# A 31-tap convolution shared by ScalarE and GpSimd inside eight attention heads, with the heads' scores one weight block later

## The chip, the cores and the metric

One Trainium2 chip (trn2), one of its cores. The metric is the device time of one execution in microseconds. Engines: PE (TensorE), DVE (VectorE), ACT (ScalarE), POOL (GpSimd) and SP (SyncE, which here only starts loads).

## The reference, cut to what matters

The input has 256 tokens of 2048 features; all is float32. `first_block` (a recurrent and attention mixer, a gated MLP, an embedding gate) runs first and the change does not touch it. `second_block` is the part in question:

```python
h = rmsnorm(x, norm_g[l])
proj = h @ w_in[l]
(cv_a, cv_b, cv_gate, fq, fk, fv, f_logit, fox_gate, mq, mem_gate) = jnp.split(proj, SPLITS, axis=-1)

u = cv_a * jax.nn.sigmoid(cv_b)                       # 512 channels
u = causal_depthwise_conv(u, conv_w[l], conv_b[l])    # 31 taps, each channel by itself
u = jax.nn.silu(layernorm(u, conv_ln_g[l], conv_ln_b[l]))
y_conv = (u @ w_conv_pw[l]) * jax.nn.silu(cv_gate)

logf = jax.nn.log_sigmoid(f_logit.astype(jnp.float32) + b_f[l].astype(jnp.float32))
y_fox = fox_attention(fq, fk, fv, logf)               # 8 heads; bias = differences of cumsum(logf)
y_fox = y_fox * jax.nn.silu(fox_gate)
y_mem = memory_attention(mq, mk, mv) * jax.nn.silu(mem_gate)      # 4 heads
y = jnp.concatenate([y_conv, y_fox, y_mem], axis=-1)
x = x + y @ w_out[l]
```

## The kernel before

Features lie on the partitions, tokens (T = 256) along the free axis. A weight block is 128 output features by 2048 inputs, 1 MB. SP loads it into one of four slots of `stage`; ACT copies it to `whi` with its high half (`hi`, L429); DVE subtracts that from the block to get `wlo` (`lo`, L834), which lies over `stage`; PE multiplies (`whole`, L1602): for each of 16 cells one matmul of `whi` with both halves of the activations (512 columns, L1586) and one of `wlo` with the high half (256 columns, L1587). The sums lie in one of two banks `ps`. ACT copies half of the bank out (`evac`, L436), DVE adds the two halves (`add`, L840, which frees the bank through `out_free`) and scales the result (`scaled`, L848 and L850). A bank is taken again two blocks later, so PE's block n waits for the `add` of block n - 2 and for `lo` of its own weights. Each engine runs its instructions in the order in which the program has them; the semaphores alone tie the engines together.

The stage around the change, in order:

- **Conv stage.** Eight blocks give cv_a and cv_b; DVE writes their gated product to `upad` (L1242, counted by `u_ready`). PE then computes the forget gate's logits with 32 small matmuls (L1837).
- **The forget gate's chain.** DVE computes log-sigmoid, cumulative sum (`cc`, L1253) and the sum's three bf16 parts (L1246 to L1262), all on 48 partitions by 256, each operation waiting for the one before (`link`). ACT does an Exp and a Ln in between (L724, L726).
- **The convolution, on POOL.** One product of `upad`, shifted by the tap, with the tap's weights, 128x1024 (`tap_product`, L1543), and one addition into `uc` (L1559), for each of 31 taps in turn (L1549 adds the convolution's bias instead after tap 0), with no one waiting for it until the memory heads.
- **Eight gate heads** (`fox_head`: ACT L737, DVE L1274, PE L1850), one block each for query, key, value and gate, i.e. blocks u to u+3. PE: block 0; turn the softmax of the head before (`fox_turned`); block 1; weighted sum of the head before (`fox_out`); block 2; the scores (`masked_scores`, L1619, which wait for the query `fqT`, the key `fkT` and the two biases `cpos` and `cneg`); block 3; turn the values (into `ps_b`). DVE: for each block `add`, `lo` of the block three ahead, `scaled`; then bias, maxima and sign of the scores (L1295 to L1298), softmax, and the gate's x * sigmoid(x) with a reciprocal of 1.75 us (`logistic`, L857). Head 0 stands alone, heads 1 to 7 are a loop.
- **Four memory heads** of two blocks each (PE L1897 on). In them the layer norm of the convolution is done piece by piece: sums by POOL and PE (`uc_summed`, `usq_summed`), mean and square on DVE after head 0, `mu` and the inverse root at head 2, scaling and gain in the middle of head 3 (L1342 to L1344), ACT's sigmoid after the last head (L793). Then four blocks for cv_gate, with turning and sum of the last memory head between them, the pointwise product (`parts`), and the 16 blocks of w_out.

Of the kernel before, what the change touches and what calls it, by code (L numbers as in the profile page):

```python
# [19 lines left out]
ALU = mybir.AluOpType  # L20
# [81 lines left out]
def build(nc, a, out):  # L102
    with ExitStack() as ctx:
# [317 lines left out]
        def _(act):  # L421
# [314 lines left out]

            def fox_head(i, before=None):  # L737
# [12 lines left out]
                act.activation(fs[:, 0:P], fs[:, 0:P], ACT.Exp, bias=cols[:, 10:11], accum_out=cols[:, 12:13]).then_inc(s("fox_exp"), 1)  # L750
                act.activation(fs[:, P:3 * P], fs[:, P:3 * P], ACT.Exp, bias=cols[:, 11:12], accum_out=cols[:, 13:14]).then_inc(s("fox_exp"), 1)
# [5 lines left out]
                act.activation(fvtok[:, :, :], ps_b.rearrange("p (a b) -> p a b", a=2), ACT.Copy).then_inc(s("fvtok_ready"), 1)  # L757

# [13 lines left out]
            for n in range(MEM_HEADS):  # L772
# [4 lines left out]
                if n == 2:  # L777
                    norm(mu[:, :], "uc")
# [46 lines left out]
        def _(dve):  # L825
# [425 lines left out]
            dve.wait_ge(s("z_ln"), 1)  # L1251
            link(dve.tensor_tensor(z2[:, :], zf[:, :], z1[:, :], ALU.subtract))
            link(dve.tensor_tensor_scan(cc[:, :], one8[:, :], z2[:, :], 0.0, ALU.mult, ALU.add))  # L1253

            for n, (whole_c, left) in enumerate(((cc, z1), (z1, z2))):
                link(dve.tensor_copy(cpart[n], whole_c[:, :]))
                link(dve.tensor_tensor(left[:, :], whole_c[:, :], cpart[n], ALU.subtract))
            keeps = [fox_rows[:, 2 * HEADS + 2 + n:2 * HEADS + 3 + n] for n in range(PARTS)]
            link(dve.tensor_scalar(cc[:, :], z2[:, :], keeps[2], None, ALU.mult))
            for n in range(2):  # L1260
                link(dve.scalar_tensor_tensor(out=cc[:, :], in0=cpart[n], scalar=keeps[n], in1=cc[:, :],
                                              op0=ALU.mult, op1=ALU.add))  # L1262


# [9 lines left out]
            def fox_head(i, before=None):  # L1274
# [5 lines left out]
                scaled(u, 0, fqT[:, :], "fq_ready", factor=SCALE)  # L1280

# [24 lines left out]
                lo(G_FOX, i, 4, 6)  # L1306
                scaled(u + 3, 1, fgx[:, :], "fg_lin")
# [23 lines left out]
            for n in range(MEM_HEADS):  # L1331
                u = U_MEM + 2 * n
                if n == 2:
                    dve.wait_ge(*event("usq_summed"))
                    dve.tensor_scalar(mu[:, :], uc_square, 1.0 / (GROUPS * P), EPS, ALU.mult, ALU.add).then_inc(event("uc_ms")[0], 1)
# [3 lines left out]
                if n == 3:  # L1339

                    dve.wait_ge(*event("uc_norm"))
                    link(dve.tensor_tensor(uc[:, :, :], uc[:, :, :], by_mean, ALU.mult))  # L1342
                    for k in range(GROUPS):
                        dve.tensor_scalar(uc[:, k, :], uc[:, k, :], column("conv_ln_g", k), column("conv_ln_b", k),  # L1344
                                          ALU.mult, ALU.add).then_inc(s("cl_ready"), 1)
# [15 lines left out]
                if n == 0:  # L1361
# [4 lines left out]
                    dve.tensor_tensor(usq[:, :, :], uc[:, :, :], uc[:, :, :], ALU.mult).then_inc(s("usq_ready"), 1)  # L1366
            dve.wait_ge(s("cl_sig"), 1)
# [51 lines left out]
        def _(pool):  # L1419
# [119 lines left out]
            pool.wait_ge(s("u_ready"), GROUPS)  # L1539
            taps = vec[:, V["taps"]:V["taps"] + GROUPS * TAPS].rearrange("p (k t) -> p k t", k=GROUPS)  # L1540
            every = [P, GROUPS, T]

            def tap_product(dst, tap):  # L1543
                return pool.tensor_tensor(dst, upad[:, :, bass.ds(tap, T)],  # L1544
                                          taps[:, :, bass.ds(tap, 1)].to_broadcast(every), ALU.mult)

            tap_product(uc[:, :, :], 0).then_inc(s("tap_done"), 1)
            pool.wait_ge(s("tap_done"), 1)
            pool.tensor_tensor(uc[:, :, :], uc[:, :, :], column("conv_b_2", 0, GROUPS).unsqueeze(2).to_broadcast(every),  # L1549
                               ALU.add).then_inc(s("tap_done"), 1)  # L1550


            with pool.Fori(0, (TAPS - 1) // 2) as i:
                chain.enter(i, 2)
                for j, made in enumerate((usq, sg_c)):
                    pool.wait_ge(s("tap_done"), 2 * i + j + 1)
                    link(tap_product(made[:, :, :], 2 * i + j + 1))
                    pool.wait_ge(s("tap_done"), 2 * i + j + 2)
                    pool.tensor_tensor(uc[:, :, :], uc[:, :, :], made[:, :, :], ALU.add).then_inc(s("tap_done"), 1)  # L1559
# [460 lines left out]
```

## Time and profile before

| | |
|---|---|
| median of 3 runs | 1953.25 us (1953.09 to 1955.03) |
| the profiled execution | 1952.65 us, span 1950.9 us |
| mean granted clock of PE | 0.969 of 2.4 GHz |
| busy: PE, DVE, ACT, POOL | 93%, 71%, 46%, 36% of the span |
| convolution and eight gate heads | 1496.6 to 1761.1 us of the span |

Busy shares are means over stages with different limits, so they are read by stretch. An instruction's duration holds what it waited for inside, for instance for a port; what an engine waited for ahead of an instruction is its idle time. The clock is given as a share of 2.4 GHz for a stretch; 0.5 is the 1.2 GHz level, and values between are mixtures.

### The profile page before, as it was taken

The numbers are of one execution on the slowest core, as the hardware profiler recorded it, in microseconds if no ns is written. First come the engines' busy times: TensorE is split into PE (matmuls) and PEld (weight loads), VectorE is DVE, ScalarE is ACT, GpSimd is POOL, SyncE is SP. The second block draws the span as 40 slices with busy tenths as digits, with TensorE's granted clock in tenths as the row PEclk, the third lists the DMA queues.
The fourth block names the chain that finished last, engine by engine and source line by source line (L and its number), as shares of the span: only waits on it lengthen the run. The fifth ranks groups of instructions, "written<-read, shape, count | busy, mean of one in ns | idle before, by whom it ended". The sixth has DMA issues, their size and how long they took to land.

```text
span 1950.9 us, 29749 instructions
## 1 busy us (share of the span) xinstructions
PE 1823.6 (93%) x10284; PEld 1586.9 (81%) x10284; DVE 1394.6 (71%) x1633; ACT 901.9 (46%) x1160; POOL 709.1 (36%) x612
## 2 busy tenths in 40 slices
PE   5899999999969999999999999997999678899997
PEld 4688888887848888888888888886887567788886
DVE  7777777876767777777777544447777887778854
ACT  4444444454346555555555433335554222345532
POOL 3444444442972111111111122223543999500033
PEclk9899999999979999999999999998999789899998
DMA  6344444445624555455555555554554233344452
GB/s 250 120 154 169 152 171 163 160 166 193 224 86 165 182 191 188 180 191 190 179 190 180 181 182 190 187 184 150 193 186 167 77 121 115 133 162 168 157 191 108
DMA packets 50424, 326.49 MB, mean 167 GB/s; under 512 B 5840, under 2 KB 6480, under 8 KB 17744
## 3 DMA queue, kind: packets, MB, share of 16 engines
q1 hardware_dynamic: 50384, 325.96, 47.1%
q8 instruction: 25, 0.41, 0.1%
q14 instruction: 15, 0.12, 0.0%
HBM read 323.84 MB, written 2.10 MB: 167 GB/s over the span
## 4 chain that ended last, share of the span: by engine, by line
PE 79%; DVE 10%; POOL 5%; issue 4%; ACT 1%; DMA 1%; DVEq 0%; POOLq 0%; SPq 0%; ACTq 0%
PE ps L1586 49%; PE ps L1587 25%; DVE wlo L834 2%; PE ps_lev L1661 1%; DVE act_a L1073 1%; POOL sq L1478 1%; PE ps_sc L1625 1%; POOL lev_in L1459 1%; POOL mem_again L1427 1%; POOL lev_in L1455 1%; DVE act_a L877 1%; DVE fqT L850 1%; DVE cpos L1283 1%; DVE fgx L848 0%; PE ps_t L1615 0%
## 5 line engine op out<-in xcount | busy, mean ns | idle before, releaser
L1586 PE MATMUL ps<-act_a,whi 128*128 128x512 f32 x3136 | 1137.3, 403 | 56.9 <-DVE tmp L840 23.9
L1587 PE MATMUL ps<-act_a,wlo 128*128 128x256 f32 x3136 | 895.3, 285 | 0.0
L834 DVE TENSOR_TENSOR wlo<-stage,whi 128x2048 fp32r<-128x2048 f32 (+1 forms) x317 | 721.2, 2275 | 229.9 <-ACT whi L429 225.6
L1586 PEld LDWEIGHTS ps<-act_a,whi 128*128 128x128 f32 x3136 | 599.6, 191 | 201.4 <-issue 34.0
L429 ACT ACTIVATE whi<-stage 128x2048 fp32r<-128x2048 f32 (+1 forms) x317 | 570.9, 1801 | 120.2 <-DMA stage<-in_w_down 108.5
L1587 PEld LDWEIGHTS ps<-act_a,wlo 128*128 128x128 f32 x3136 | 600.8, 192 | 0.9
L1586 PE MATMUL ps<-big,whi 128*128 128x512 f32 x1600 | 569.2, 397 | 8.2 <-DVE big L1164 6.9
L1587 PE MATMUL ps<-big,wlo 128*128 128x256 f32 x1600 | 454.7, 284 | 0.0
L436 ACT ACTIVATE small<-ps 128x256 f32<-128x256 f32 x252 | 96.2, 382 | 592.5 <-PE ps L1587 592.3
L1586 PEld LDWEIGHTS ps<-big,whi 128*128 128x128 f32 x1600 | 303.2, 190 | 79.2 <-DVE big L1164 5.2
L1587 PEld LDWEIGHTS ps<-big,wlo 128*128 128x128 f32 x1600 | 303.6, 190 | 0.1
L840 DVE TENSOR_TENSOR tmp<-ps,small 128x256 f32<-128x256 f32 x212 | 89.6, 422 | 198.9 <-ACT small L436 192.0
L1521 POOL TENSOR_TENSOR upb<-tmp,rstd 128x256 f32<-128x256 f32 x88 | 76.5, 870 | 414.5 <-DVE tmp L840 400.3
L1455 POOL TENSOR_TENSOR lev_in<-qq,pfx 128x128 f32<-128x128 f32 x64 | 47.6, 744 | 221.6 <-DVE qq L979 217.2
L1479 POOL TENSOR_TENSOR acc<-acc,sq 128x256 f32<-128x256 f32 x63 | 100.2, 1590 | 5.0
L1478 POOL TENSOR_TENSOR sq<-y 128x256 f32 x16 | 11.7, 730 | 195.5 <-DVE y L840 195.5
L1478 POOL TENSOR_TENSOR sq<-h 128x256 f32 x31 | 19.0, 613 | 164.4 <-DVE h L1402 116.2
L1100 DVE SCALAR_TENSOR_TENSOR cy<-upb,vec,cy 128x256 f32<-128x256 f32 x88 | 64.4, 732 | 12.5 <-DVE cy L1098 12.2
L605 ACT ACTIVATE cy<-upb,vec 128x256 f32<-128x256 f32 x88 | 52.5, 596 | 4.0 <-POOL upb L1521 4.0
L1459 POOL TENSOR_TENSOR lev_in<-kk,sfx 128x128 f32<-128x128 f32 x64 | 49.1, 767 | 5.0
L1463 POOL TENSOR_TENSOR pfx<-pfx 128x128 f32<-128x128 f32 x56 | 46.9, 837 | 4.4
L1559 POOL TENSOR_TENSOR uc<-uc,usq 128x1024 f32<-128x1024 f32 x15 | 46.0, 3068 | 2.4 <-POOL usq L1544 2.4
(326 smaller groups left out, 1433.1 us busy)
## 6 DMA issues: line engine op xcount, KB each, us to landing
stage<-in_w_a SPq DMA_DIRECT2D x167, 1024.0 KB, 4.8
stage<-in_w_b SPq DMA_DIRECT2D x87, 1024.0 KB, 4.8
stage<-in_w_down SPq DMA_DIRECT2D x64, 704.0 KB, 4.0
h<-in_xT SPq DMA_DIRECT2D x8, 512.0 KB, 6.5
mem_raw<-in_memT SPq DMA_DIRECT2D x1, 2048.0 KB, 10.7
mem_again<-in_memT SPq DMA_DIRECT2D x4, 512.0 KB, 7.5
out<-o_out SPq DMA_DIRECT2D x4, 512.0 KB, 2.7
stage<-in_w_a SPq DMA_DIRECT2D x4, 256.0 KB, 7.0
```

The lines of the kernel that those rows point to most:

```text
L429: act.activation(whi[:, slot, 0:cells * P], stage[:, slot, 0:cells * P], ACT.Copy).then_inc(w_hi, 1)
L436: act.activation(small[:, b, :], ps[:, b, T:2 * T], ACT.Copy).then_inc(small_ready, 1)
L605: act.activation(cy[:, b, :], upb[:, b, 2:T + 2], ACT.Identity, scale=w[0], bias=w[1])\
L834: dve.tensor_tensor(wlo[:, slot, part], stage[:, slot, part], whi[:, slot, part].bitcast(F32), ALU.subtract).then_inc(w_lo, 1)
L840: dve.tensor_tensor(tmp[:, b, :] if dst is None else dst, ps[:, b, 0:T], small[:, b, :], ALU.add).then_inc(out_free, 1)
L1100: dve.scalar_tensor_tensor(out=cy[:, b, :], in0=upb[:, b, 0:T], scalar=w[0], in1=cy[:, b, :], op0=ALU.mult, op1=ALU.add).then_inc(s(done), 1)
L1455: link(pool.tensor_tensor(x1, q1, p1, ALU.mult))
L1459: pool.tensor_tensor(x0, k0, s0, ALU.mult).then_inc(s("lev_in_ready"), 1)
L1479: pool.tensor_tensor(total, total, sq, ALU.add).then_inc(step(done + "_acc", 0)[0], 1)
L1521: pool.tensor_tensor(upb[:, q % 2, 2:T + 2], tmp[:, q % 2, :], rstd[:, :], ALU.mult).then_inc(s("up_ready"), 1)
L1586: pe.matmul(ps[:, bank, :], whi[:, slot, c * P:(c + 1) * P], act, start=start, stop=False)
L1587: return pe.matmul(ps[:, bank, T:2 * T], wlo[:, slot, c * P:(c + 1) * P], act[:, 0:T], start=False, stop=stop)
```

## The change

- The convolution's products go to ACT: `first_taps` (tap 0 with the bias, four Identity activations of 128x256), then `tap_products`, four Copy activations of 128x256 each scaled by a column of weights, into `sg_c` and `usq` by turns. Two taps are made in head 0, four in each of the seven turns of the loop. POOL only adds (`add_tap`), each tap in two halves of 128x512. POOL waits for `product_made`; ACT waits for `product_added` before it overwrites a buffer of two taps ago.
- PE runs all four blocks of a head ahead of its scores; turning and sum of the head before come one block later. ACT and DVE follow that order.
- On DVE the softmax goes ahead of the gate's reciprocal and product, `add` and `scaled` of block 3 go ahead of the scores' bias and maxima, and the split of the head before goes behind the softmax. On ACT the softmax's exponentials go behind the block's high half, the gate's exponential and the values' copy.
- The second part of the forget gate's chain (`forget_gate`) goes behind the first `add`, `lo` and `scaled` of head 0.
- The convolution's mean is taken after memory head 1 instead of 0, the inverse root in head 3 instead of 2, and scaling and gain come behind the last memory head instead of in its middle. PE's column sums move with them.

```diff
             def fox_head(i, before=None):          # ACT
                 u = U_FOX + 4 * i
                 evac(u, 0, G_PG - U_PG)
                 hi(G_FOX, i, 4, 3)
-                if before is not None:
-                    fox_turned(before)
+                if before is None:
+                    first_taps()
+                else:
+                    tap_products(before, 3)
                 evac(u + 1, 1, G_PG - U_PG)
                 hi(G_FOX, i, 4, 4)
+                if before is None:
+                    tap_products(0, 1)
+                else:
+                    fox_turned(before)
+                    tap_products(before, 4)
                 evac(u + 2, 0, G_PG - U_PG)
                 hi(G_FOX, i, 4, 5)
-                if before is not None:
+                if before is None:
+                    tap_products(0, 2)
+                else:
                     fox_out(before)
-                wait(act, "fox_max", i + 1)
...
+                    tap_products(before, 5)
                 evac(u + 3, 1, G_PG - U_PG)
                 hi(G_FOX, i, 4, 6)
                 wait(act, "fg_lin", i + 1)
                 act.activation(fge[:, :], fgx[:, :], ACT.Exp, scale=-1.0).then_inc(s("fg_exp"), 1)
...
+                wait(act, "fox_max", i + 1)
...
+                if before is not None:
+                    tap_products(before, 6)
```

```diff
+            def first_taps():
+                act.wait_ge(s("u_ready"), GROUPS)
+                for k in range(GROUPS):
+                    act.activation(uc[:, k, :], upad[:, k, 0:T], ACT.Identity, scale=tap_column(0, k),
+                                   bias=column("conv_b_2", k)).then_inc(s("product_made"), 1)
+
+            def tap_products(i, j):
+
+                made = (sg_c, usq)[j % 2]
+                if not (isinstance(i, int) and j <= 2):
+                    act.wait_ge(s("product_added"), i * 8 + 2 * (j - 2))
+                for k in range(GROUPS):
+                    act.activation(made[:, k:k + 1, :], upad[:, k:k + 1, bass.ds(4 * i + j, T)], ACT.Copy,
+                                   scale=tap_column(4 * i + j, k)).then_inc(s("product_made"), 1)
...
+            def add_tap(i, j):                     # POOL
+
+                made = (sg_c, usq)[j % 2]
+                for half in range(2):
+                    pair = slice(2 * half, 2 * half + 2)
+                    pool.wait_ge(s("product_made"), i * 16 + 4 * j + 2 * half + 2)
+                    if not (isinstance(i, int) and j == 1):
+                        pool.wait_ge(s("product_added"), i * 8 + 2 * (j - 1) + half - 1)
+                    pool.tensor_tensor(uc[:, pair, :], uc[:, pair, :], made[:, pair, :], ALU.add).then_inc(s("product_added"), 1)
+
+            add_tap(0, 1)
+            add_tap(0, 2)
+            with pool.Fori(0, HEADS - 1) as n:
+                for j in range(3, 7):
+                    add_tap(n, j)
```

```diff
             def fox_head(i, before=None):          # DVE
...
                 scaled(u, 0, fqT[:, :], "fq_ready", factor=SCALE)
+                if before is None:
+                    forget_gate()
...
                 if before is not None:
                     fox_gated(before)
+                add(u + 3, 1)
+                scaled(u + 3, 1, fgx[:, :], "fg_lin")
                 wait(dve, "fsc_ready", i + 1)
                 wait(dve, "fp_turned", i)
                 link(dve.tensor_tensor(fs[:, 0:3 * P], ps_sc[:, 0:3 * P], bias_fox, ALU.add))
...
-                if before is not None:
-                    fox_split(before)
-                add(u + 3, 1)
+                lo(G_FOX, i, 4, 6)
                 wait(dve, "fox_exp", 2 * i + 2)
...
-                lo(G_FOX, i, 4, 6)
-                scaled(u + 3, 1, fgx[:, :], "fg_lin")
+                if before is not None:
+                    fox_split(before)
                 logistic(fge[:, :], "fg_exp", i + 1)
```

```diff
             def fox_head(i, before=None):          # PE
                 u = U_FOX + 4 * i
                 whole(G_FOX, i, 4, 0, u, 0, act_a)
+                whole(G_FOX, i, 4, 1, u + 1, 1, act_a)
                 if before is not None:
                     fox_turned(before)
-                whole(G_FOX, i, 4, 1, u + 1, 1, act_a)
+                whole(G_FOX, i, 4, 2, u + 2, 0, act_a)
                 if before is not None:
                     fox_out(before)
-                whole(G_FOX, i, 4, 2, u + 2, 0, act_a)
+                whole(G_FOX, i, 4, 3, u + 3, 1, act_a)
                 wait(pe, "c_ready", 2 * i + 2)
...
-                whole(G_FOX, i, 4, 3, u + 3, 1, act_a)
```

```diff
+            dve.wait_ge(*event("uc_norm"))         # DVE, behind the last memory head
+            link(dve.tensor_tensor(uc[:, :, :], uc[:, :, :], by_mean, ALU.mult))
+            for k in range(GROUPS):
+                dve.tensor_scalar(uc[:, k, :], uc[:, k, :], column("conv_ln_g", k), column("conv_ln_b", k),
+                                  ALU.mult, ALU.add).then_inc(s("cl_ready"), 1)
             dve.wait_ge(s("cl_sig"), 1)
             dve.tensor_tensor(uc[:, :, :], uc[:, :, :], usq[:, :, :], ALU.mult).then_inc(s("cs_ready"), 1)
```

## Rows read from the trace of the kernel before

**Rows 1.** The page: engine totals, as busy us, share of the span, instructions.

```profile
PE 1823.6 (93%) x10284; PEld 1586.9 (81%) x10284; DVE 1394.6 (71%) x1633; ACT 901.9 (46%) x1160; POOL 709.1 (36%) x612
```

**Rows 2.** By stretch: length; busy (count) PE, PEld, DVE, ACT, POOL; clock; DMA.

```profile
1496.70:1539.00 42.30, 21.36 (x103) 17.73 (x104) 41.84 (x25) 9.83 (x10) 41.11 (x17) 0.76 0.20 75
1539.00:1573.50 34.50, 28.30 (x145) 23.73 (x144) 27.97 (x25) 10.68 (x15) 33.55 (x12) 0.90 0.34 122
...
1705.30:1730.40 25.10, 25.10 (x145) 21.71 (x144) 17.86 (x26) 11.04 (x17) 0.00 (x0) 1.00 0.43 164
...
1539.00:1678.40 139.40, 112.86 (x574) 94.64 (x573) 115.70 (x103) 43.68 (x63) 135.92 (x45) 0.89 0.34 121
...
1496.70:1761.20 264.50, 217.03 (x1138) 183.96 (x1139) 213.60 (x211) 87.53 (x124) 183.77 (x64) 0.90 0.35 123
```

**Rows 3.** Waits, 1489 to 1700 us: who for whom, total, times, longest.

```profile
PE ps_sc L1624 <- DVE fkT L848: 22.7, 5, 5.2
...
PE ps L1586 <- DVE tmp L840: 22.4, 5, 16.9
```

**Rows 4.** DVE by line, a slow head (1573.5 to 1608.6), then a quiet one.

```profile
L834 DVE TENSOR_TENSOR wlo<-stage,whi 128x2048 fp32r<-128x2048 f32 x4 | 12.4, 3112 | 0.0
...
L840 DVE TENSOR_TENSOR tmp<-ps,small 128x256 f32<-128x256 f32 x4 | 1.7, 417 | 5.3 <-ACT small L436 4.7 <-DVE fge L1309 0.6
...
L834 DVE TENSOR_TENSOR wlo<-stage,whi 128x2048 fp32r<-128x2048 f32 x4 | 9.2, 2290 | 3.3 <-ACT whi L429 3.3
```

**Rows 5.** DVE in order of time, the forget gate's chain: start, duration.

```profile
1497.16 0.39 DVE L1247 TENSOR_SCALAR zf<-zf,bfox 48x256 f32<-48x256 f32 x1
...
1504.02 2.01 DVE L1252 TENSOR_TENSOR z<-zf,z 48x256 f32<-48x256 f32 x1
```

**Rows 6.** PE in order of time: first cells of the first and third block.

```profile
1496.61 0.50 PE L1586 MATMUL ps<-act_a,whi 128*128 128x512 f32 x1
...
1525.02 0.76 PE L1586 MATMUL ps<-act_a,whi 128*128 128x512 f32 x1 [16.93 <-DVE tmp L840]
```

**Rows 7.** POOL in order of time.

```profile
1541.24 2.38 POOL L1559 TENSOR_TENSOR uc<-uc,sg_c 128x1024 f32<-128x1024 f32 x1 [0.16 <-POOL sg_c L1544]
1543.57 1.91 POOL L1544 TENSOR_TENSOR usq<-upad,vec 128x1024 f32 x1
...
1567.73 8.28 POOL L1559 TENSOR_TENSOR uc<-uc,usq 128x1024 f32<-128x1024 f32 x1 [0.16 <-POOL usq L1544]
...
1683.35 1.29 POOL L1563 TENSOR_TENSOR sg_c<-uc 128x512 f32<-128x512 f32 x1
```

**Rows 8.** The chain that ended last, in order of time: scores of two heads.

```profile
1704.09 0.42 PE ps_sc L1625 x2
...
1754.20 0.42 PE ps_sc L1625 x2
```

**Rows 9.** ACT's activations of 128x256: two page rows, one line of the stage before.

```profile
L436 ACT ACTIVATE small<-ps 128x256 f32<-128x256 f32 x252 | 96.2, 382 | 592.5 <-PE ps L1587 592.3
...
L605 ACT ACTIVATE cy<-upb,vec 128x256 f32<-128x256 f32 x88 | 52.5, 596 | 4.0 <-POOL upb L1521 4.0
...
L688 ACT ACTIVATE act_a<-h,vec x16: 496/498/511, 1367.8 to 1450.5; - x12, 128x256 fp32r<-128x256 f32 x4
```

**Rows 10.** After the last memory head: DVE, ACT and PE in order of time.

```profile
1812.72 1.22 DVE L1342 TENSOR_TENSOR uc<-uc,mu 128x1024 f32<-128x1024 f32 x1
1813.97 1.38 DVE L1344 TENSOR_SCALAR uc<-uc,vec 128x256 f32<-128x256 f32 x4
...
1822.58 0.42 DVE L1360 TENSOR_TENSOR fge<-fge,fgx 128x256 f32<-128x256 f32 x1
...
1819.91 1.07 ACT L793 ACTIVATE usq<-uc 128x1024 f32<-128x1024 f32 x1
...
1823.99 0.58 ACT L766 ACTIVATE fpT<-ps_t 128x512 f32<-128x512 f32 x1
...
1827.75 0.59 PE L1887 MATMUL bank_a<-fpT,fvtok 128*128 128x256 f32 x2
```

More of the change, by code:

```diff
@@ L735, in fox_out, with tap_column @@
                 act.activation(xs_y[:, bass.ds(GROUPS + n, 1), 0:T], fo[:, :].unsqueeze(1), ACT.Copy).then_inc(s("fo_hi"), 1)
+            def tap_column(tap, k):
+                return vec[:, bass.ds(V["taps"] + k * TAPS + tap, 1)]
+            def first_taps():
[10 more added lines that the diff above has]
+                                   scale=tap_column(4 * i + j, k)).then_inc(s("product_made"), 1)
             def fox_head(i, before=None):
@@ L757, in fox_head @@
                 act.activation(fvtok[:, :, :], ps_b.rearrange("p (a b) -> p a b", a=2), ACT.Copy).then_inc(s("fvtok_ready"), 1)
+                wait(act, "fox_max", i + 1)
+                act.activation(fs[:, 0:P], fs[:, 0:P], ACT.Exp, bias=cols[:, 10:11], accum_out=cols[:, 12:13]).then_inc(s("fox_exp"), 1)
+                act.activation(fs[:, P:3 * P], fs[:, P:3 * P], ACT.Exp, bias=cols[:, 11:12], accum_out=cols[:, 13:14]).then_inc(s("fox_exp"), 1)
+                if before is not None:
+                    tap_products(before, 6)
             fox_head(0)
@@ L776, in _ @@
                 memory_turned(n - 1) if n else fox_turned(HEADS - 1)
-                if n == 2:
+                if n == 3:
                     norm(mu[:, :], "uc")
@@ L1250, in _, with forget_gate @@
             link(dve.tensor_scalar(zf[:, :], zf[:, :], 0.0, None, ALU.min))
[L1251 to L1262, printed above, removed]
+            def forget_gate():
+                dve.wait_ge(s("z_ln"), 1)
+                link(dve.tensor_tensor(z2[:, :], zf[:, :], z1[:, :], ALU.subtract))
+                link(dve.tensor_tensor_scan(cc[:, :], one8[:, :], z2[:, :], 0.0, ALU.mult, ALU.add))
+                for n, (whole_c, left) in enumerate(((cc, z1), (z1, z2))):
+                    link(dve.tensor_copy(cpart[n], whole_c[:, :]))
+                    link(dve.tensor_tensor(left[:, :], whole_c[:, :], cpart[n], ALU.subtract))
+                keeps = [fox_rows[:, 2 * HEADS + 2 + n:2 * HEADS + 3 + n] for n in range(PARTS)]
+                link(dve.tensor_scalar(cc[:, :], z2[:, :], keeps[2], None, ALU.mult))
+                for n in range(2):
+                    link(dve.scalar_tensor_tensor(out=cc[:, :], in0=cpart[n], scalar=keeps[n], in1=cc[:, :],
+                                                  op0=ALU.mult, op1=ALU.add))
             def fox_gated(n):
@@ L1332, in _ @@
                 u = U_MEM + 2 * n
-                if n == 2:
+                if n == 3:
                     dve.wait_ge(*event("usq_summed"))
@@ L1338, in _ @@
                 lo(G_MEM, 0, 0, 2 * n + 3)
[L1339 to L1345, printed above, removed]
                 add(u + 1, 1)
@@ L1536, in _ @@
                              lambda i: pool.wait_ge(s("h3_ready"), i + 1), "h3", None)
[L1539 to L1559, printed above, removed]
-                chain.leave((TAPS - 1) // 2)
-            pool.wait_ge(s("tap_done"), TAPS + 1)
+            def add_tap(i, j):
[11 more added lines that the diff above has]
+                    add_tap(n, j)
+            pool.wait_ge(s("product_added"), 2 * (TAPS - 1))
             link(pool.tensor_tensor(sg_c[:, 0:2, :], uc[:, 0:2, :], uc[:, 2:4, :], ALU.add))
@@ L1903, in _ @@
                 turn(ps_b[:, P:T], mkv[:, MEM_HEADS + n, P:T], "mv_turned")
-                if n == 1:
+                if n == 0:
+                    column_sums(ps_lev[:, 0, 0, :], [sg_c[:, 2, :]], lambda n: event("uc_sum"), "uc_summed")
+                if n == 2:
                     column_sums(ps_lev[:, 1, 0, :], [usq[:, 0, :]], lambda n: event("usq_sum"), "usq_summed")
```

5 lines of the change are left out of this document (1 added, 4 removed).

## The prediction, made before the change was run

> **What bounds the kernel now.** Start with the page's engine totals [rows 1]: PE is busy for 93% of the span, so a change pays only where PE waits or runs slow. Next read busy time and clock by stretch [rows 2]. From 1496.7 to 1761.2 us eight gate heads run. A head in its quiet form (1705.3 to 1730.4) takes 25.1 us, PE is busy in all of it, the granted clock is 1.00 (2.4 GHz), and POOL does nothing. Four heads before it take 34.5 to 35.1 us (139.4 in all; the first is shown), with the clock at 0.89 to 0.90 and POOL busy nearly throughout: that is the convolution. The first 42.3 us are worse, PE busy for 21.4 and the clock at 0.76. Third, the waits [rows 3]: PE waits for two things, fkT (what the scores need, 22.7 us) and DVE's additions out of the output bank (22.4 us, 16.9 of it at once). DVE in its turn stands 5.3 us in a slow head for ScalarE's copy out of the bank [rows 4], which waits for PE. So the two take turns: PE stands before the scores, then the fourth block runs, then DVE stands until it is done.
>
> Why is DVE late? In the four slow heads it is busy 115.7 us where four quiet heads make 4 x 17.9 = 71.4 [rows 2]: 44.3 us are waiting inside instructions. The gate's chain shows it most plainly [rows 5]: an operation on 48x256 takes 0.39 us with POOL idle and 2.01 with POOL at work, and from 1504.0 until the addition that frees PE at 1525.0 [rows 6] the gate's cumulative sum and splits hold DVE. POOL's instructions in these heads are an addition of 2.38 us and a product of 1.91 by turns [rows 7]. 22 of each is 94 us of POOL's own work, so each microsecond of it costs DVE 44.3/94 = 0.47.
>
> What perfect heads would save. The quiet period is (1754.20 - 1704.09)/2 = 25.06 us [rows 8]. Seven of those, and a head 0 that has nothing to turn or sum for a predecessor (about 1.0 us less), make 199.5 us. The stage takes 264.5 [rows 2]. The difference, **65.0 us**, is 47.5 of PE idle (264.5 - 217.0) and about 17.5 of slow clock [rows 2]. A quiet head keeps PE busy all the time, so this is the ceiling, and no reordering below can gain beyond it. The loads keep up: a quiet head has the same four of 1 MB in 25.1 us, at a DMA share of 0.43 [rows 2].
>
> **The change part by part.**
>
> *Products to ScalarE.* POOL loses 31 products and the bias addition, and keeps 30 additions, each in two halves of 128x512. A half should take 1.29 us, what the one addition of that size took [rows 7]; half of a whole one, 1.19, is the lower bound, and waiting comes on top (up to the 5.9 us of the third rival). A loop turn holds eight: 10.3 us of POOL instead of all of it. At 0.47 that costs DVE 4.8 us a head, so DVE needs 17.9 + 4.8 = 22.7 of 25.1 us. ScalarE gains 16 products a head. No row has such an operation in this stage; the nearest is a Copy scaled by a column, 0.50 us [rows 9]. 16 x 0.50 = 8.0 on top of 11.0 [rows 2] makes 19.0 of 25.1. The bounds are 0.38 (a plain copy of this width) and 0.60 (scaled and biased by columns) [rows 9]: 17 to 21 us, which fits either way. What waits behind them on ScalarE is an evacuation. A block takes about 5.7 us (two from 1496.6 to 1508.1 [rows 6]); evacuation 0.3, high half 1.9, products 1.6 to 2.0 make 3.8 to 4.2, so the next evacuation is not late. Cost: **0**, covered by PE; without that cover up to 8 us a head.
>
> *The scores a block later.* PE now runs all four blocks and then the scores, so keys and cumulative sum have 5.7 us more, and DVE no longer stands behind the fourth block. PE's work is the same. In return the softmax's DVE work of head i reaches into the first block of head i+1. Counted from the start of a head: the fourth block ends at 23.3, scores at 24.6; DVE's parts, all of them within its 17.9: bias, maxima and sign 1.8 -> 26.4; low half 2.2 (2.29 with the overlap taken off [rows 4]) -> 28.6; softmax and split 1.3 -> 29.9; gate 2.5 -> 32.4; the first addition of the next head is possible at 31.1 and so done at 32.8. PE needs it for its third block, at 36.7. Of the 3.9 us in hand POOL can take two half additions (2.6). Further on the slacks are similar: the second addition done at 41 at worst against 42.7, the low half for the next head 43 against 50. The turning of the old head's weights also moves a block later, with the wait of ScalarE (fpT) and PE (output): weights ready at 29.5, needed at 36.7. Cost: **0**.
>
> *Softmax ahead of the sigmoid; products and ScalarE's exponentials reordered.* The same work by the same instructions. ScalarE's exponentials now stand behind the next high half and the values' copy (about 2.8 us after the evacuation at 23.3), which is when the maxima are ready. Cost 0.
>
> *The gate's chain into head 0.* Ten linked operations. They no longer delay the first addition, since that comes before them, and POOL cannot start before ScalarE has made two products of tap 1. PE's first block ends at 1502.2 as before; evacuation, high half and four first products carry ScalarE to 1506.5, second evacuation and high half to 1510.3, so POOL starts at about 1511.2. DVE: addition 1503.1, low half to 1506.7, fqT 1507.1, then ten times 0.45 (0.42 and a gap) = 4.5 -> 1511.6, biases 0.7 -> 1512.3, second addition 1512.7. PE needs it at 1513.5. With two half additions of POOL in between it is 1515.3. The unhindered price of the scan stands in no row; it can be 0.4 like its neighbours or 2.8 as it was with POOL in the way. I take a stall of **1.5 us** there, with 0 and 4 as ends (4 if PE drops to its 1.2 GHz level there, as the 0.76 of this stretch shows it did [rows 2]).
>
> *The norm moved back.* Mean and square one memory head later cost nothing: they fill gaps of DVE like those they leave. But the scaling now stands behind the last memory head's gate, at 1823.0: 1.2 + 1.4 us [rows 10] -> 1825.6, then ScalarE's sigmoid 1.1 -> 1826.7 (before, it ran at 1819.9 [rows 10]). Behind it wait the evacuation (possible at about 1822), a high half of 1.9 and the turned weights of the last head, ready at 1829.4 instead of 1824.6. PE wants them at 1827.8 [rows 10]. Cost: **+1.6 us**, ends 0 and 4. The pointwise product's input is done near 1837 and wanted at 1841: covered by the two blocks that remain.
>
> Sum: -65.0 + 1.5 + 1.6 = **-62 us**. Against the profiled execution (1952.65 us with a span of 1950.9) that is 1890.7; the median shown is 0.6 above it, so 1891.
>
> **The rivals.**
>
> *DVE becomes the bound.* If POOL's halves fall on DVE in full, a head costs 17.9 + 10.3 = 28.2 us instead of 25.1. Seven heads: 22, less 4 of slack = 18 more, 1909; a PE that waits also drops to its lower level, which adds up to 1.6 us each time. For it: the halves are released just when ScalarE has made a high half, and that is when DVE starts its low half of 2.3 us. Against it: the measured 0.47, and DVE's reads of the banks, which showed no waiting (0.417 us in a slow head, where a low half had grown from 2.29 to 3.11) [rows 4]. The Trainium skill (SBUF — State Buffer, Who interferes with whom) says the shared port pair is held for a whole instruction by whoever comes first and the other blocks fully. That is this rival's rule; by it alone the sum would be 1909, by the rows 1891.
>
> *The order of PE and DVE is good but the convolution still drags.* Heads at about 30 us, the slow ones' mean of 34.9 less PE's wait for fkT (22.7 / 5 = 4.5 [rows 3]): (30.4 - 25.1) x 7 = 37, 1928. It would need POOL's new load to weigh as much as the old, for which I see no row.
>
> *Slower than before.* POOL can be kept out: five of its instructions took over 8 us instead of 1.9 or 2.4, such as the one at 1567.7 [rows 7], about 5.9 us of waiting while DVE ran back to back. ScalarE now waits for POOL (product_added) with high halves and evacuations queued behind, so a starved addition reaches PE. 60 half additions in 264.5 us is 4.4 us each: from that mean on the kernel is slower than before. If each waited 5.9 us the stage would take 60 x 7.2 = 432 us, 167 more, about 2120. Against: a tap may be late by a whole block before ScalarE stops, and DVE has gaps in every block of a quiet head, where POOL gets in.
>
> **How the numbers follow.** PE-bound heads, 1887 to 1898: 60%. DVE-bound heads, 1898 to 1915: 26%. Heads dragged, 1915 to 1949: 9%. Within 0.2% of before: 2%. Slower: 3%. 0.2% is about what a measurement of this kernel tells from no change. The range 1886 to 1914 takes in the first two, 85%, and all ends of the unknown terms. Faster 95%, same 2%, slower 3%.
>
> **What would show it.** Right: head period near 25.1 with the clock at 1.00 from head 1 on; DVE busy 22 to 23 us and ScalarE 19 per head; POOL's halves near 1.3 us with a few longer; scores of head 0 near 1520 and the stage done near 1697 to 1698; gate operations of 0.4 us; a PE wait of about 1.6 us at the last memory head's output. Wrong: a period of 27 to 28 with DVE never idle (first rival); long POOL halves with ScalarE waiting for them (third). A saving above 66 us would mean that I missed something outside this stage.

## The result

The changed kernel takes **1902.2 us** (median of 4 runs, 1902.0 to 1903.0) where the kernel before, run again on the same chip, takes 1953.7 (1953.1 to 1955.0): ratio 0.9736, 95% interval 0.9719 to 0.9753. That is 51.5 us less. The forecast was 1891, 62 less; the time lies inside its range of 1886 to 1914, but some 11 us of the gain are missing, and the question of the rest of this text is where they went.

The profiled execution took 1903.01 us, with a span of 1901.2. The page's totals, beside [rows 1]:

```profile
PE 1812.0 (95%) x10284; PEld 1578.2 (83%) x10284; DVE 1357.9 (71%) x1633; ACT 951.9 (50%) x1284; POOL 629.0 (33%) x610
```

Busy time by stretch, with the columns of [rows 2]: head 0, heads 1 and 2, one period among the five later heads, the first memory head.

```profile
1496.70:1521.50 24.80, 24.80 (x140) 20.77 (x138) 18.04 (x27) 15.53 (x24) 9.85 (x4) 1.00 0.41 133
1521.50:1546.80 25.30, 25.30 (x146) 21.84 (x146) 19.47 (x25) 15.99 (x30) 9.66 (x6) 1.00 0.45 165
1546.80:1573.50 26.70, 25.37 (x145) 21.70 (x144) 23.46 (x27) 17.53 (x33) 10.62 (x9) 1.00 0.45 158
...
1599.51:1625.97 26.46, 25.31 (x144) 21.64 (x143) 22.33 (x26) 17.42 (x33) 13.69 (x9) 1.00 0.42 157
...
1705.80:1723.10 17.30, 14.94 (x78) 12.88 (x78) 15.50 (x20) 9.15 (x16) 6.29 (x6) 0.90 0.33 118
```

The stage that took 264.5 us [rows 2] takes 208.6 (1497.1 to 1705.7). Its clock is 1.00 throughout, and there is no wait for the key any more [rows 3]. But from head 2 on a head takes 26.5 us and not 25.1, and PE is idle in it for 1.2. What it waits for, in order of time on PE (start, duration; in brackets idle time before it and what ended it); two of the six such waits, then the one in the first memory head with cells behind it, then one after the last:

```profile
1559.59 0.50 PE L1610 MATMUL ps<-act_a,whi 128*128 128x512 f32 x1 [1.33 <-DVE tmp L870]
...
1612.59 0.50 PE L1610 MATMUL ps<-act_a,whi 128*128 128x512 f32 x1 [1.15 <-DVE tmp L870]
...
1713.74 0.90 PE L1639 MATMUL ps_t<-ident,fs 128*128 128x128 f32 x3 [2.36 <-DVE fs L1338]
...
1715.09 0.63 PE L1610 MATMUL ps<-act_a,whi 128*128 128x512 f32 x1
...
1717.00 0.39 PE L1610 MATMUL ps<-act_a,whi 128*128 128x512 f32 x1
...
1777.96 0.67 PE L1911 MATMUL bank_a<-fpT,fvtok 128*128 128x256 f32 x2 [1.52 <-issue]
```

`L870` is `add`: from head 2 on the third block of each head waits for DVE's first addition of that head. These waits of 1.15 to 1.33 us leave the clock at 1.00. The cells after the wait of 2.36 us at 1713.7 take 0.63 us each until 1717, with the clock at 0.50, the 1.2 GHz level. The addition's evacuation was done long before. This is DVE in order of time, from block 3's addition of one head to the first addition of the next:

```profile
1623.34 0.41 DVE L1298 TENSOR_TENSOR fo<-bank_a,fge 128x256 f32<-128x256 f32 x1
1626.21 0.42 DVE L870 TENSOR_TENSOR tmp<-ps,small 128x256 f32<-128x256 f32 x1 [2.45 <-ACT small L436]
1626.67 1.42 DVE L878 TENSOR_TENSOR fgx<-tmp,rstd 128x256 f32<-128x256 f32 x1
...
1631.86 1.13 DVE L1337 TENSOR_SCALAR fs<-fs,cols 128x128 f32<-128x128 f32 x1
1632.91 1.40 DVE L1338 TENSOR_SCALAR fs<-fs,cols 128x256 f32<-128x256 f32 x1
...
1634.88 1.75 DVE L887 RECIPROCAL fge<-fge 128x256 f32<-128x256 f32 x1
1636.67 1.36 DVE L1342 TENSOR_TENSOR fge<-fge,fgx 128x256 f32<-128x256 f32 x1
1638.57 0.42 DVE L870 TENSOR_TENSOR tmp<-ps,small 128x256 f32<-128x256 f32 x1 [0.53 <-ACT small L436]
```

and ScalarE, then POOL, in the same stretch (an `x2` of POOL is the two halves of one tap):

```profile
1623.90 0.42 ACT L735 ACTIVATE big<-fo 128x256 f32 x1 [3.13 <-DVE fo L1298]
1624.22 1.69 ACT L752 ACTIVATE usq<-upad,vec 128x256 f32 x4
1625.82 0.36 ACT L436 ACTIVATE small<-ps 128x256 f32<-128x256 f32 x1
...
1632.08 0.38 ACT L436 ACTIVATE small<-ps 128x256 f32<-128x256 f32 x1
...
1625.27 2.53 POOL L1578 TENSOR_TENSOR uc<-uc,usq 128x512 f32<-128x512 f32 x2 [4.55 <-ACT usq L752]
1631.51 2.65 POOL L1578 TENSOR_TENSOR uc<-uc,sg_c 128x512 f32<-128x512 f32 x2 [3.71 <-ACT sg_c L752]
1635.22 2.53 POOL L1578 TENSOR_TENSOR uc<-uc,usq 128x512 f32<-128x512 f32 x2 [1.06 <-ACT usq L752]
```

DVE first stands idle for 2.45 us, because PE now does block 3 ahead of the scores and nothing else stands ahead of that block's addition in DVE's program. The block ends at 1624.7, and a copy out of the bank (L436) can follow 0.1 us behind a block's end, as the one at 1637.69 does. But this one comes only at 1625.8, 1.0 us late: four products (tap 5) stand ahead of it on ScalarE, and they stand behind a copy of `fo` for which ScalarE had waited 3.13 us. Then DVE has fourteen instructions in a row, and four of them, each beside a POOL addition, take 1.42, 1.13, 1.40 and 1.36 us. In head 0 the same kind of scaled product took 0.41 (`fkT`), and the other three, standing clear of POOL, took 0.29, 0.35 and 0.42. That is 3.8 us of waiting inside. DVE's L1338, for one, ends at 1634.31, 0.15 us after POOL's tap at 1634.16. The turn of the loop adds 0.5: the profile names ScalarE for it, which had been done since 1632.5, but the same 0.53 us stand there in the second experiment, where another instruction comes first. So the addition that was possible at 1632.5 is made at 1638.6.

### The profile page after: what moved, and what is told of

It reads as the page before. It is cut to its first block, busy times and chain, and to the rows that moved or that the text cites. A ratio compares the mean times of both kernels' runs of the same rounds, so it can differ in the third digit from the quotient of the medians.

```text
span 1901.2 us, 30010 instructions
## 1 busy us (share of the span) xinstructions
PE 1812.0 (95%) x10284; PEld 1578.2 (83%) x10284; DVE 1357.9 (71%) x1633; ACT 951.9 (50%) x1284; POOL 629.0 (33%) x610
## 4 chain that ended last, share of the span: by engine, by line
PE 80%; DVE 8%; POOL 5%; issue 4%; ACT 2%; DMA 1%; DVEq 0%; POOLq 0%; ACTq 0%; SPq 0%
PE ps L1610 50%; PE ps L1611 26%; PE ps_lev L1685 1%; POOL sq L1509 1%; DVE act_a L1103 1%; DVE wlo L864 1%; POOL mem_again L1458 1%; POOL lev_in L1490 1%; POOL lev_in L1486 1%; DVE act_a L907 1%; DVE fge L887 1%; DVE fs L1338 1%; ACT whi L429 0%; POOL sfx L1493 0%; DVE tmp L870 0%
## 5 line engine op out<-in xcount | busy, mean ns | idle before, releaser
L864 DVE TENSOR_TENSOR wlo<-stage,whi 128x2048 fp32r<-128x2048 f32 (+1 forms) x317 | 711.4, 2244 | 227.0 <-ACT whi L429 222.6
L436 ACT ACTIVATE small<-ps 128x256 f32<-128x256 f32 x252 | 96.4, 382 | 540.3 <-PE ps L1611 540.2
L870 DVE TENSOR_TENSOR tmp<-ps,small 128x256 f32<-128x256 f32 x212 | 89.4, 421 | 190.4 <-ACT small L436 185.6
L1578 POOL TENSOR_TENSOR uc<-uc,usq 128x512 f32<-128x512 f32 x30 | 42.9, 1451 | 110.0 <-ACT usq L752 110.0
L1578 POOL TENSOR_TENSOR uc<-uc,sg_c 128x512 f32<-128x512 f32 x30 | 59.8, 2013 | 48.3 <-ACT sg_c L752 48.3
```

What stands on the lines that cost most here:

```text
L436: act.activation(small[:, b, :], ps[:, b, T:2 * T], ACT.Copy).then_inc(small_ready, 1)
L864: dve.tensor_tensor(wlo[:, slot, part], stage[:, slot, part], whi[:, slot, part].bitcast(F32), ALU.subtract).then_inc(w_lo, 1)
L870: dve.tensor_tensor(tmp[:, b, :] if dst is None else dst, ps[:, b, 0:T], small[:, b, :], ALU.add).then_inc(out_free, 1)
L1578: pool.tensor_tensor(uc[:, pair, :], uc[:, pair, :], made[:, pair, :], ALU.add).then_inc(s("product_added"), 1)
```

## The experiments

All are compared with the kernel before on the same chip; times are medians, and the head period is the distance of the same matmul in neighbouring heads. First three tests of what makes the first addition late, and one half of the change by itself.

**POOL's additions made small** (most of the convolution's sum left out):

```diff
-pool.tensor_tensor(uc[:, pair, :], uc[:, pair, :], made[:, pair, :], ALU.add)
+pool.tensor_tensor(uc[:, pair, 0:2], uc[:, pair, 0:2], made[:, pair, 0:2], ALU.add)
```

> The changed kernel with POOL's sixty additions cut to 2 of 256 columns each (most of the convolution's sum is left out; products, waits and order stay). Theory L (late chain): heads take 26.5 us instead of 25.1 because DVE's chain from block 3's evacuation to the next head's first addition is too long, 3.9 us of it waits for POOL's port. Without them: period 25.1, DVE busy 17.9 a head, 6 x 1.4 = 8.5 us saved and 1 to 2 at the first memory head, 1892 +- 2. Theory D (DVE's load as a whole is the bound): the same 25.1. Theory S (ScalarE's longer program is the bound): period stays 26.5, 1902.

Measured 1889.6 (0.967, 0.9654 to 0.9686), 12.6 us less than the change. One head:

```profile
1596.05:1621.12 25.07, 25.07 (x144) 21.63 (x144) 17.71 (x26) 17.38 (x33) 5.14 (x8) 1.00 0.46 167
```

PE is never idle, DVE is busy for 17.7 us, and ScalarE as long as before (17.4). S falls: the longer program of ScalarE alone costs nothing. What remains is POOL's use of the port, by its place (L) or by its sum (D).

**The next head's first addition ahead of split and gate:**

```diff
+                add(u + 4, 0)
                 if before is not None:
                     fox_split(before)
                 logistic(fge[:, :], "fg_exp", i + 1)
```

(with the head's own `add(u, 0)` left to head 0, and that of memory head 0 left out.)

> The changed kernel with one DVE instruction moved: the first addition of the next head goes ahead of the old head's split and gate (about 3.5 us earlier). L: the chain to that addition is shorter by 3.5 us, which is more than the 1.4 it is late, so period 25.1 to 25.3, DVE busy unchanged at 22.3, total 1894 +- 2. D: DVE's load is the same, period stays at 26.5, 1902. S: 1902.

Measured 1900.4 (0.9728, 0.9712 to 0.9744): next to nothing. The lateness went one place further. PE, and the window from one such wait to the next:

```profile
1668.46 0.50 PE L1613 MATMUL ps<-act_a,whi 128*128 128x512 f32 x1 [0.90 <-DVE tmp L870]
```

```profile
1642.24:1668.46 26.22, 25.32 (x143) 21.71 (x144) 22.98 (x27) 17.45 (x33) 10.71 (x8) 1.00 0.45 160
```

It is now the head's fourth block that waits, for the second addition, and the period is 26.2. L as I had it, one late instruction, is wrong. And the wait in the first memory head grew from 2.36 to 3.14 us, which takes back part of what the heads gained.

**Tap 5's products behind block 3's evacuation and high half:**

```diff
                     fox_out(before)
-                    tap_products(before, 5)
                 evac(u + 3, 1, G_PG - U_PG)
                 hi(G_FOX, i, 4, 6)
+                if before is not None:
+                    tap_products(before, 5)
```

> The changed kernel with ScalarE's four products of tap j = 5 put behind block 3's evacuation and high half, instead of ahead. L: the evacuation comes 0.9 us earlier, so the chain does, period 25.6, 6 x 0.9 = 5 us and up to 1 more at the first memory head: 1897 +- 2. D: 1902, as the load is the same.

Measured 1900.5 (0.9727, 0.9711 to 0.9743), and all of it outside the heads: PE's wait in the first memory head fell from 2.36 to 0.57 us, while the period stayed at 26.5. The evacuation did come earlier, but tap 5's additions, which had fallen partly into DVE's idle time, now met the softmax and the gate, so the chain lost on DVE what it gained on ScalarE:

```profile
1633.22 1.51 DVE L1303 TENSOR_TENSOR big<-fo,big 128x256 f32 x1
1634.66 1.38 DVE L887 TENSOR_SCALAR fge<-fge 128x256 f32<-128x256 f32 x1
```

**Order of the heads alone**, the convolution all on POOL as before (gate's chain and norm in the change's places).

> The changed kernel with the convolution as before, all on POOL; order of the heads, place of the gate's chain and of the norm as in the change. If the order removes the turns that PE and DVE take: five or six slow heads at about 30 us instead of 34.8, first head 8 us shorter, 1922 +- 6. If the order only helps where POOL is light: heads stay at 34 to 35, 1945 or more.

Measured 1937.3 (0.9916, 0.99 to 0.9933): 16.7 less than before, halfway between my two numbers. A slow head takes 30.1 to 30.7 us instead of 34.8, PE and DVE no longer take turns, and DVE is nearly full, busy for 28.5 of 30.2 us:

```profile
1616.60:1646.76 30.16, 27.09 (x143) 22.94 (x144) 28.53 (x27) 11.00 (x16) 29.37 (x10) 0.94 0.39 142
```

But head 0 gained little: PE waited 20.6 us for the second addition, because the gate's chain now stood ahead of that one, with POOL at work.

**The shared convolution alone**, heads and gate's chain in the old order, norm in its new place: PE, DVE and ScalarE run `fox_head` as the kernel before has it, with `tap_products` after the first, second and third high half and at the end.

> The kernel before with only the convolution shared by ScalarE and POOL and the norm moved back; heads and the gate's chain in the old order. In quiet heads of before the key was ready 1.2 us ahead of the scores, and POOL's halves now cost DVE 2 to 3 us ahead of it. Expected: PE waits 1 to 2 us for the key in each of seven heads, period 26.5 to 27.5, the gate's chain undisturbed (operations of 0.4 us), total 1906 +- 5. If the order of the heads is what carries the gain: above 1925.

Measured **1896.1** (0.971, 0.9693 to 0.9727), 6 us better than the whole change. The old order's wait for the key is 0.5 us in most heads, 1.0 in one and nothing in another:

```profile
1643.21 0.21 PE L1646 MATMUL ps_sc<-cneg,cpos 48*128 48x128 bf16 x1 [0.52 <-issue]
```

```profile
1617.59:1643.21 25.62, 25.11 (x143) 21.67 (x144) 20.76 (x26) 17.16 (x33) 14.77 (x9) 1.00 0.44 164
```

So the parts don't add: order alone -16.7, sharing alone -57.7, both -51.5 (each with the norm in its new place; the order includes the gate's chain in its new place). With the convolution on POOL the new order is worth 17 us; with it shared, it costs 6. I had expected neither sign nor size.

**POOL's additions whole** (one of 128x1024 a tap instead of two halves), in the changed kernel.

> The changed kernel with POOL's additions whole (128x1024, one per tap instead of two halves). L with a port held per instruction: a DVE instruction that meets one waits up to 2.4 us instead of 1.3, but half as often, and the addition starts only after all four products (0.8 us later). POOL's own work is the same, so DVE busy stays 21.5 to 22.5 a head and the time within 1902 +- 3. If what counts is the longest single wait: period over 27, 1906 or more.

Measured 1916.7 (0.9815, 0.9797 to 0.9832): the second of the two answers. The heads take 27.9 to 29.5 us, the longer ones in part at the lower clock (0.94 to 0.95 in them). One of the short ones:

```profile
1650.36:1678.44 28.08, 25.31 (x144) 21.65 (x144) 24.85 (x27) 17.41 (x34) 10.39 (x4) 1.00 0.42 151
```

**POOL's additions in quarters** (four of 128x256), in the changed kernel.

> The changed kernel with POOL's additions in four pieces of 128x256 for each tap instead of two of 128x512. One addition of 128x256 took 0.74 us in the kernel before, so POOL has 4 x 0.74 = 3.0 us of its own work a tap instead of 2.5. Whole additions made the head 28 to 29 us. If the length of a single wait is what makes DVE late: a wait of at most 0.75 us, DVE busy 21 a head, period 25.1 to 25.6, 1895 +- 2. If the number of meetings counts as much: DVE as busy as with halves (22.3), period 26.5, 1902 +- 1.5; if POOL's total work decides: over 1904.

Measured 1892.8 (0.969, 0.9674 to 0.9706), 9.4 us better than halves and near the first of the three answers. PE waits 0.33 us in every second head. Two heads:

```profile
1585.23:1635.94 50.71, 50.38 (x287) 43.30 (x287) 41.23 (x53) 34.75 (x65) 30.79 (x32) 1.00 0.46 165
```

Undisturbed, whole, halved (the change) and quartered additions cost POOL 2.4, 2.6 and 3.0 us a tap; with the first experiment they make a row. DVE busy in a head: 17.7 us with additions of two columns (0.2 us at the shortest, the row below), 20.6 with quarters, 22.3 with halves, 24.9 with whole ones. What DVE loses, 2.9, 4.6 and 7.1 us, grows with the length of a single addition (0.74, 1.3, 2.4 us) and not with POOL's sum, which falls from quarters to whole ones. The first experiment's row for half of its additions, nanoseconds as shortest, median and longest:

```profile
L1578 POOL TENSOR_TENSOR uc<-uc,usq x30: 201/216/3055, 1512.5 to 1697.5; 128x4 f32<-128x4 f32 x30
```

**Turning and sum of the last gate head a step later** in memory head 0 (PE's part):

```diff
-                memory_turned(n - 1) if n else fox_turned(HEADS - 1)
+                if n:
+                    memory_turned(n - 1)
                 whole(G_MEM, 0, 0, 2 * n + 1, u + 1, 1, act_a)
-                memory_out(n - 1) if n else fox_out(HEADS - 1)
+                memory_out(n - 1) if n else fox_turned(HEADS - 1)
...
+                if n == 0:
+                    fox_out(HEADS - 1)
```

> The changed kernel with one thing moved in memory head 0: the last gate head's softmax is turned after block 1 and its weighted sum taken after the memory scores, as the change does in gate heads. Theory: PE now waits there for DVE's softmax 2.4 us and loses 1.1 more to its 1.2 GHz level; both go: 1899 +- 1, granted clock 1.00 in the first memory head. Rival: the wait only moves to the next thing that DVE does late (query or addition of memory head 0): 1902.

Measured 1900.5 (0.9733, 0.9716 to 0.9751). The wait of 2.36 us is gone, and one of 1.44 for DVE's query (`DVE fqT`) ahead of the memory scores is there instead: between my two answers. The gain of 1.7 is inside the interval.

**The sigmoid behind the next evacuation**, high half and turned weights; DVE's product with it behind the first gate block's addition:

```diff
-            act.wait_ge(s("cl_ready"), GROUPS)
-            act.activation(usq[:, :, :], uc[:, :, :], ACT.Sigmoid).then_inc(s("cl_sig"), 1)
...
                     memory_turned(MEM_HEADS - 1)
+                    act.wait_ge(s("cl_ready"), GROUPS)
+                    act.activation(usq[:, :, :], uc[:, :, :], ACT.Sigmoid).then_inc(s("cl_sig"), 1)
```

> The changed kernel with ScalarE's sigmoid of the convolution put behind the next evacuation, high half and turned weights, and DVE's product with it behind the first gate block's addition. Theory: PE's wait of 1.5 us at the last memory head's sum goes: 1900.5 +- 0.7. Rival: the pointwise product's input comes so much later that PE waits for it instead: 1902 or more.

Measured 1900.5 (0.9732, 0.9715 to 0.975). The 1.52 us wait at the last memory head's sum is in no row of this run; the place is shown, the 1.7 us are within the interval. DVE's part of the edit is not in the cut above.

**The gate's chain in its new place, with the old order of the heads and the shared convolution.**

> The kernel with the shared convolution and the heads in the old order, and now the forget gate's second part in the place where the change has it (behind head 0's first addition, low half and query). With POOL idle while the chain runs in its old place, the place is worth nothing: 1896 +- 1.5. If the place carried part of the gain: 1893 or less, if it delays the key of head 0: 1898 or more.

Measured 1897.7 (0.9712, 0.9697 to 0.9727) against 1896.1: no gain from the place. PE's wait for the key of head 0 grew from 0.51 to 2.29 us. Once POOL starts later than the chain, there is nothing to protect it from.

**Four moves at once in the new order**: the first addition ahead, tap 5 behind the evacuation, the later turning, the sigmoid behind.

> The changed kernel with four things moved at once: the next head's first addition ahead of split and gate, tap 5's products behind block 3's evacuation, the last turning a block later, the sigmoid behind the next evacuation. Theory C (the cycle): with the scores behind all four blocks DVE stands before block 3's addition and then has all its work for the head in one piece, so a single move only hands the lateness to the next addition; the period stays at 26 to 26.3 and only the places outside the gate heads mend: 1896 +- 2. If the moves add up in the heads too: period 25.1 to 25.5, 1891 or less.

Measured **1889.9** (0.9675, 0.966 to 0.969), 12.3 us better than the change and the best of the kernels that compute the whole convolution. My theory C, that moves only hand the lateness on, is wrong too. PE has no wait in heads 1 to 7; one head:

```profile
1596.71:1621.78 25.07, 25.07 (x145) 21.63 (x144) 23.12 (x27) 17.27 (x33) 15.31 (x8) 1.00 0.46 166
```

DVE is busy for 23.1 of the 25.1 us, more than in the changed kernel, and still in time. So D, DVE's load as a whole, is out as well.

```profile
1603.39 0.41 DVE L874 TENSOR_TENSOR tmp<-ps,small 128x256 f32<-128x256 f32 x1
1603.73 1.18 DVE L1306 TENSOR_TENSOR big<-fo,big 128x256 f32 x1
1604.84 1.38 DVE L890 TENSOR_SCALAR fge<-fge 128x256 f32<-128x256 f32 x1
...
1613.65 0.41 DVE L874 TENSOR_TENSOR tmp<-ps,small 128x256 f32<-128x256 f32 x1
```

The first addition stands ahead of the two waits for the port that the single move of tap 5 had put in front of it. The second addition, for which PE had waited 0.9 us when the first alone was moved, now comes 18.3 us after the scores' start instead of 20.0: block 3 is copied out earlier, and its scaled product takes 0.42 us and no longer 1.42. It is done at 1614.1, and the fourth block starts at 1614.7. As I read it, two deadlines were missed by about a microsecond each, and each move mended one. That the two moves inside the heads do it, and not the two outside, follows from where they act; the pair wasn't run by itself.

**The same mending in the old order**: sigmoid behind, the convolution's sum on PE a block later, tap 5 behind block 3's evacuation.

> The kernel with the shared convolution and the heads in the old order, with three small moves: the convolution's sigmoid behind the next evacuation (1.5 us of PE's wait), PE's sum of the convolution one block later (0.9 us), tap 5's products behind block 3's evacuation and high half (evacuation 1.1 us earlier; the head's wait of 0.5 us goes if that was its cause). Theory C: 1891.5 +- 1.5, period 25.1 to 25.6. If tap 5's additions do harm in their new place, as they did in the new order: 1894 +- 1.

Measured 1906.8 (0.9764, 0.975 to 0.9777), 10.7 us worse than without the three, and far above both answers. Of them only tap 5 lies in the heads, and the heads are what got longer (26.9 to 29.9 us, at a clock of 0.95); tap 5 wasn't moved by itself. DVE, on its way to the key that the scores wait for:

```profile
1609.06 1.51 DVE L880 TENSOR_TENSOR fgx<-tmp,rstd 128x256 f32<-128x256 f32 x1
...
1611.07 0.82 DVE L888 TENSOR_SCALAR fge<-fge 128x256 f32<-128x256 f32 x1 [0.49 <-ACT fge L785]
...
1613.71 1.39 DVE L1341 TENSOR_TENSOR fge<-fge,fgx 128x256 f32<-128x256 f32 x1
...
1618.17 1.52 DVE L882 SCALAR_TENSOR_TENSOR fqT<-tmp,rstd 128x256 f32<-128x256 f32 x1
1619.61 1.38 DVE L1315 TENSOR_SCALAR cpos<-cc,fox_rows 48x256 bf16<-48x256 f32 x1
```

Five waits in that chain. Before the move the same five instructions took 0.42, 0.29, 0.66, 1.53 and 1.38 us: 2.3 us less in all. And tap 5's additions had begun at a moment when DVE stood idle for 1.4 us, and cost it 0.3:

```profile
1624.21 2.81 POOL L1576 TENSOR_TENSOR uc<-uc,usq 128x512 f32<-128x512 f32 x2 [4.34 <-ACT usq L752]
```

The same move helped in one order, beside the first addition's, and went with a loss in the other. By these rows what decides is which DVE instructions the additions meet, and whether PE waits for these.

## Why the prediction was right, and where it was wrong

**The time fell into the second class of the forecast.** 1902 lies in the class "DVE-bound heads, 1898 to 1915", given 26%, and not in the one with 60%, "PE-bound heads". The range holds it because it takes in both.

**The ceiling held.** It said that at most 65 us were to be had. The best complete kernel here has 63.7 (1953.6 - 1889.9) with a head period of 25.07, where 25.06 was forecast.

**DVE's cost of POOL held as a sum, in part by luck.** Forecast: 0.47 us per microsecond of POOL's own work, so 4.8 a head and DVE at 22.7. Measured: 22.33, where it is 17.86 with POOL idle [rows 2]. But 0.47 is no constant of the kernel: against the 17.7 us of the first experiment, quarters cost DVE 0.25 us per microsecond of POOL's own work, halves 0.45 and whole additions 0.74. Nothing here shows why the mean of the kernel before should fit the halves; I count it as luck. ScalarE's products were cheaper than assumed, 1.70 us for four, and it is busy for 17.4 and not 19 us a head. The first experiment shows that this cost nothing by itself.

**The step that failed is the cost of 0 for the scores a block later.** The prediction followed this very chain, from the fourth block to the first addition at "32.8 against 36.7", and found 3.9 us in hand, of which POOL could take 2.6. It took 3.8: six halves are released while the chain runs, and four of its instructions each met one, where the sum had allowed for two. The evacuation was 1.0 late because of tap 5's products. The prediction had reckoned ScalarE by its load, 3.8 to 4.2 us a block, and not with the 3.13 us for which it stands before `fo`, ahead of these products. And the turn of the loop took 0.5. Together 5.3 against 3.9, so 1.4 us a head; measured are waits of PE of 1.15 to 1.33 us and a period of 26.5 instead of 25.1, and 8.9 us over the seven periods (184.3 against 175.4). The average of 0.47 was used for the load, but a chain has to be priced with what can meet it. And the rule that was put down as the first rival's fits better than I allowed: the Trainium skill (SBUF — State Buffer, Who interferes with whom) says that the one who comes second blocks fully, until the instruction ends. The trace agrees: the four instructions waited 0.84 to 1.05 us each, and quarters, halves and whole additions cost 2.9, 4.6 and 7.1 us a head. The rival's sum, all of POOL's 10.3 us on DVE, did not come: 4.6 did, since some halves ran where DVE stood idle or was in an instruction that did not slow down, as the reciprocal, which took 1.75 us with a half beside it and without.

It also missed what the new order takes away. In the old order the scores come ahead of the fourth block, so DVE has softmax and gate to do while that block runs. In the new one it stands for 2.45 us and then has them all in one piece. The prediction counted PE's gain from this order and called its price 0.

**The first memory head was left out.** There the last gate head's turning still comes after one block and not two, as PE's new order has it elsewhere; the softmax was not ready. From its first block to the next head's it took 17.6 us, where the first experiment, without this wait, took 13.6. These 4.0 us, 2.36 of them idle and the rest mostly cells at the lower clock, had no term in the sum.

**Head 0: forecast 1.5 us of waiting, measured none.** The gate's operations took 0.28 to 0.50 us and the scan 0.68. A half addition did get in the way once (`cpos`, 1.26 us), but the second addition was done at 1513.8, just in time for the fourth block at 1514.0; with a second half in the way it would have been late. The forecast of the scores at about 1520 was right (1519.7).

**The norm moved back: forecast 1.6, measured 1.52** of idle time, at the named place, by the named path.

The sum is then: 62 forecast, less 8.9 for the periods, less 4.0, plus 1.5 = 50.6. Measured are 51.5 between the medians and 49.7 between the spans of the two profiled executions.

**The rivals.** The first (DVE becomes the bound) came nearest in time, 1909 against 1902 where the forecast said 1891, but its mechanism was only half right: DVE is not full in any head, at 22.3 of 26.5 us. It is late at one point. The third needed additions of 4.4 us in the mean and did not come near: 30 of them took 1.45 us, 30 took 2.01.

**Attribution.** The forecast gave the gain to both parts in one sum. The runs give it all to the sharing, which is worth 57.7 us alone (with the norm's new place), and the new order as it stands takes 6 of them back; with its two moves inside the heads it is the best run here. The gate's place shows no gain: 1.6 us the other way, with executions that overlap.

## What to carry over

When two engines share a port, price the contention twice: as a mean for the load, and, for a chain that has a deadline, by counting the instructions of the other engine that can be released while it runs, each at its full length. Cut the side instructions short and release them where the other engine stands idle; here their sum mattered less than their length and place. Before an order is changed to remove a wait, look at which work ran under the block that moves, and test the parts of a change one by one: two good parts here made a worse kernel than one, until the second was mended.

## What the runs showed that was not expected

- Additions in quarters cost POOL more (0.74 us each, 3.0 a tap, against 2.4 whole), but DVE 2.9 us a head instead of 7.1.
- The port's waits lie in POOL's time too. An addition of two columns takes 0.2 us, but up to 3.06 where DVE is at work, and eight of them stood for 5.14 us in one head while DVE lost nothing measurable (17.71 us against 17.86 with POOL idle). So the time in which POOL's instruction stands in the profile is not the time in which it keeps DVE out.
- POOL can be held off for long: in the changed kernel the row below has two halves that took 5.97 us together, where undisturbed ones take 1.28 each. DVE had seven instructions back to back in that time. No engine waited for it.

```profile
1614.75 5.97 POOL L1578 TENSOR_TENSOR uc<-uc,sg_c 128x512 f32<-128x512 f32 x2 [3.46 <-ACT sg_c L752]
```
